# Sums of squares over 512 rows by split fp32r products instead of fp32 column products, in six norms of a two-block transformer kernel

## The reference

```
def rmsnorm(x, g):                      # EPS = 1e-6; the second block has EPS_2 = 1e-5
    x32 = x.astype(jnp.float32)
    y = x32 * lax.rsqrt(jnp.mean(x32 * x32, axis=-1, keepdims=True) + EPS)
    return (y * g.astype(jnp.float32)).astype(x.dtype)
...
x = x + jnp.concatenate([mix_out, mem_out], axis=-1) @ w_out
x = x + conv_ffn(rmsnorm(x, norm_ffn_g[l]), ffn_w_up[l], ffn_conv_w[l], ffn_conv_b[l], ffn_w_down[l])
...
def conv_ffn(h, w_up, conv_w, conv_b, w_down):
    u, g = jnp.split(h @ w_up, 2, axis=-1)
    g = causal_dwconv(g, conv_w, conv_b)
    return (jax.nn.silu(g) * u) @ w_down
```

## Time and profile before

| | us |
|---|---|
| runs | 1776.76, 1777.09, 1777.13; median 1777.09 |
| span of the profiled execution | 1775.3 |
| median less that span | 1.8 |
| TensorE (PE) busy | 1765.4 (99%) |
| VectorE (DVE) busy | 1273.6 (72%) |
| ScalarE (ACT) busy | 949.8 (53%) |
| GpSimd (POOL) busy | 204.9 (12%) |

### The profile page before, as it was taken

One profiled execution on the slowest core, in us unless ns is written; L12 is line 12 of the kernel. 1 busy time (PEld: TensorE's weight loads), 2 busy tenths in 40 slices (PEclk: granted clock), 3 DMA queues, 4 the chain that ended last, 5 costly groups with the idle time before them and its releaser, 6 DMA issues.

```text
span 1775.3 us, 26378 instructions
## 1 busy us (share of the span) xinstructions
PE 1765.4 (99%) x10758; PEld 1534.0 (86%) x10758; DVE 1273.6 (72%) x1773; ACT 949.8 (53%) x1440; POOL 204.9 (12%) x225
## 2 busy tenths in 40 slices
PE   9999999999999999999999999999999999999998
PEld 7877788999999887777899999978777889999997
DVE  6878567788786655656888787687767487766765
ACT  6645444655555544755555555552567455454454
POOL 0001220110111200002011110103001101111110
PEclk9999999999999999999999999999999999999999
DMA  6221223554545333212364554433221235555442
GB/s 249 72 92 64 71 95 107 152 138 139 143 123 139 103 132 110 96 48 85 107 173 114 154 129 141 109 119 106 73 96 48 97 106 145 141 140 145 107 140 74
DMA packets 61623, 205.19 MB, mean 116 GB/s; under 512 B 7344, under 2 KB 9520, under 8 KB 53184
## 3 DMA queue, kind: packets, MB, share of 16 engines
q1 hardware_dynamic: 38832, 162.55, 26.5%
q0 software_dynamic: 17280, 31.46, 10.0%
q10 hardware_dynamic: 5392, 9.51, 1.7%
HBM read 169.38 MB, written 2.13 MB: 97 GB/s over the span
## 4 chain that ended last, share of the span: by engine, by line
PE 96%; DVE 2%; ACT 1%; DMA 0%; SPq 0%; issue 0%; DVEq 0%; ACTq 0%
PE ps L1784 31%; PE ps L1451 21%; PE ps L1810 16%; PE ps L1373 7%; PE ps L1470 4%; PE ps L1833 2%; PE ps L1490 2%; PE ps L1597 2%; PE ps L1642 2%; PE ps L1622 2%; PE ps L1681 1%; PE ps L1662 1%; PE ps L1851 1%; PE ps L1414 1%; PE ps L1353 0%; DVE WL L2449 0%
## 5 line engine op out<-in xcount | busy, mean ns | idle before, releaser
L1784 PE MATMUL ps<-hH,WL 128*128 128x256 f32 x896 | 253.6, 283 | 0.0
L1784 PE MATMUL ps<-hL,WH 128*128 128x256 f32 x896 | 253.6, 283 | 0.0
L1784 PE MATMUL ps<-hH,WH 128*128 128x256 f32 x896 | 253.4, 283 | 0.0
L2471 DVE TENSOR_TENSOR WL<-raw,WH 128x1024 fp32r<-128x1024 f32 x138 | 168.3, 1221 | 116.6 <-ACT WH L1935 116.6
L2449 DVE TENSOR_TENSOR WL<-raw,WH 128x1024 fp32r<-128x1024 f32 (+1 forms) x138 | 167.6, 1253 | 91.8 <-ACT WH L1924 91.7
L1451 PE MATMUL ps<-hH,WH 128*128 128x512 f32 x544 | 215.3, 396 | 0.0
L1451 PE MATMUL ps<-hH,WL 128*128 128x512 f32 x544 | 212.0, 390 | 0.0
L1451 PE MATMUL ps<-hL,WH 128*128 128x512 f32 x544 | 211.9, 390 | 0.0
L3197 POOL DMA_DIRECT2D X<-sq x120 | 104.9, 967 | 862.0 <-ACT sq L1990 860.1
L1784 PE MATMUL ps<-TH,WL 128*128 128x256 f32 x672 | 190.2, 283 | 0.0
L1784 PE MATMUL ps<-TL,WH 128*128 128x256 f32 x672 | 190.2, 283 | 0.0
(11 more groups left out here) (418 smaller groups left out, 3869.0 us busy)
## 6 DMA issues: line engine op xcount, KB each, us to landing
raw<-in_wall SPq DMA_DIRECT2D x166, 512.0 KB, 4.2
raw<-in_wall SPq DMA_DIRECT2D x65, 1024.0 KB, 4.7
X<-sq POOLq DMA_DIRECT2D x120, 256.0 KB, 4.0
bias<-in_bias ACTq DMA_DIRECT2D x12, 256.0 KB, 2.9
raw<-in_wall SPq DMA_DIRECT2D x8, 256.0 KB, 6.1
X<-in_xt SPq DMA_DIRECT2D x8, 256.0 KB, 6.7
CB<-rows ACTq DMA_DIRECT2D x8, 256.0 KB, 3.4
out_y<-X SPq DMA_DIRECT2D x8, 256.0 KB, 2.2
```

Source lines behind the costliest of these rows:

```text
L1784: mm = e.matmul(ps[b][:, 256 * u:256 * u + 256], ww[:, p, 128 * u:128 * u + 128], x, start=(opens and p == 0 and u == 0 and n == 0), stop= ...
L2471: e.tensor_tensor(L, chunk_src(c), H.bitcast(F32), ALU.subtract).then_inc(*mark("wl", "c", c))
```

## The change

Six norms lose their column products. `acc` is split into a high and a low fp32r part (`row_split`: ScalarE copies `accH`, VectorE subtracts for `accL`), and TensorE multiplies a 128x128 tile of ones, `ones_r`, with both, summed in one bank of 128x512 (`row_sums`). ScalarE takes the root over 128x512 straight into Rsb, and VectorE the reciprocal of Rsb in place (`row_inverse`). Where columns are needed (mix0, kv, n1), VectorE makes them from Rsb: four products with the identity, each with a sum along the free axis (`row_columns`). The spreads and the copy of Rsb are gone. The accH and accL tiles lie where sq0 and sq1 do.

The order changes too. In the feed-forward parts the split takes the place of the old sums, and the new sums come after g1; the reciprocal follows at once (WHOLE 2) or after the next conversions (WHOLE 1). For kv the three steps fall on three tiles one after another, without the pause ahead of them. In mix0 the split lies between the halves of the conversion of unit 3. At the join both splits come before the first tile of dq, the sums after dq1 with one root and reciprocal, the second reciprocal and the columns after the second piece of dv.

```diff
     def rstd(i, eps):
-        norms.extend([None, ("rstd_rows", i, eps), None] if i in ("ffn0", "ffn1", "n2") else
-                     [None, ("rstd_first", i, eps), ("rstd_second", i)])
+        norms.extend([("row_split", i), ("row_sums", i, eps), ("row_inverse", i)])
...
         whole("g", 0, n)
-        put("rstd_first", st, 61 if i == 2 else 60)
+        put("row_split", st)
         put("wtS", i, 1)
         put("wtL", i, 1)
         put("wtB", i, 2)
         put("wtS", i, 2)
         whole("g", 1, n)
         done.add(n)
-        put("rstd_second", st)
+        put("row_sums", st, 61 if i == 2 else 60)
+        if WHOLE[i] == 2:
+            put("row_inverse", st)
...
         conv_ahead(len(UNITS))
+        if WHOLE[i] == 1:
+            put("row_inverse", st)
...
+    put("conv", 3, 0)
+    put("row_split", "mix0")
+    put("conv", 3, 1)
+    now["conv"] = 4
     tm(1, "memA", "mvA", "mvcp", ntt=2)
     put("gate_products", "A")
-    put("rstd_first", "mix0", 60)
-    norms.append(("rstd_second", "mix0"))
+    put("row_sums", "mix0", 60)
+    put("row_inverse", "mix0")
...
-    norms.extend([None, ("join_first",), ("join_second",)])
+    norms.extend([None, ("join_sums",), ("join_second",)])
     put("fence", "C")
     put("rope_load")
     put("chunk_bias")
+    put("join_split")
...
+            def row_sums(b, parts, key):
+                for n, x in enumerate(parts):
+                    mm = e.matmul(ps[b][:, :], ones_r[:, :], x[:, :], start=(n == 0), stop=(n == 1))
                 mm.then_inc(*mark(*key))
...
+                elif what == "row_split":
+                    w.wait_ge(*at("acc" + SQ_LAST[a[0]], a[0], 7))
+                    e.activation(accH[:, :], acc[:, :], ACT.Copy).then_inc(*mark("rowH", a[0]))
...
                     e.activation(Rsb[:, :], ps[BANK[("rs", a[0])]][:, :], ACT.Sqrt, bias=small[:, eps:eps + 1],
                                  scale=1.0 / 1024).then_inc(*mark("rsq", a[0]))
...
+            def row_low(low, whole, high, name):
+                w.wait_ge(*at("rowH", name))
+                e.tensor_tensor(low[:, :], whole[:, :], high[:, :].bitcast(F32), ALU.subtract).then_inc(
+                    *mark("rowL", name))
+            def row_columns(name):
...
+                for i in range(4):
+                    c = slice(128 * i, 128 * i + 128)
+                    e.tensor_tensor_reduce(diag[:, c], Rsb[:, c], ident, 1.0, 0.0, ALU.mult, ALU.add,
+                                           small[:, 4 + i:5 + i]).then_inc(*mark("rcol", name, i))
...
+                elif what == "row_inverse":
                     w.wait_ge(*at("rsq", a[0]))
+                    e.reciprocal(Rsb[:, :], Rsb[:, :]).then_inc(*mark("Rsb", a[0]))
+                    if a[0] in ("mix0", "kv"):
+                        row_columns(a[0])
...
+                elif what == "join_split":
+                    row_low(accL, acc, accH, "n1")
+                    row_low(acc2L, acc2, acc2H, "join")
+                elif what == "join_sums":
+                    w.wait_ge(*at("sums", "n1"))
+                    w.wait_ge(*at("sums", "join"))
+                    e.tensor_scalar(Rsb[:, :], ps[BANK[("rs", "n1")]][:, :], 1e-5, None, ALU.mult).then_inc(
+                        *mark("jsq1"))
+                    w.wait_ge(*at("jsq1"))
+                    e.tensor_tensor(Rsb[:, :], Rsb[:, :], ps[BANK[("rs", "join")]][:, :], ALU.add).then_inc(
+                        *mark("jsq"))
                     w.wait_ge(*at("rsq", "n1"))
+                    e.reciprocal(Rsb[:, :], Rsb[:, :]).then_inc(*mark("Rsb", "n1"))
+                elif what == "join_second":
                     w.wait_ge(*at("rsq", "join"))
+                    e.reciprocal(acc2[:, :], acc2[:, :]).then_inc(*mark("Rsb", "join"))
+                    row_columns("n1")
```

More of the change, by code:

```diff
@@ L1024, in program @@
         K = place("K", [128, 5, 128])
+        ones_r = place("ones_r", [128, 128], F32R)
         KB = place("KB", [128, 3, 128], BF16)
@@ L1028, in program @@
         diag = place("diag", [128, 512])
+        accH, accL = (place(f"acc{x}", [128, 512], F32R, offset=top[0] - 2048 * n) for x, n in (("H", 3), ("L", 2)))
         held_w = place("held3", [128, 2, 256], offset=top[0] - 2048)
@@ L1138, in program @@
         Tf = place("Tf", [128, 4, 256], offset=wino + 49152)
+        acc2H, acc2L = (place(f"acc2{x}", [128, 512], F32R, offset=wino + 81920 + 2048 * n)
+                        for n, x in enumerate("HL"))
         gw = place("gw", [128, 8, 32], offset=227840)
@@ L1526, in tensor @@
                         w.wait_ge(*at(*before))
-                    w.wait_ge(*at("acc" + SQ_LAST[a[0]], a[0], 7))
-                    sums(b, acc, 0, ("sums", a[0]))
-                elif what == "rstd_rows":
-                    b, before = bank(("rs", a[0]), ("rsq", a[0]))
-                    if before:
-                        w.wait_ge(*at(*before))
[L1535 to L1557, removed]
+                    w.wait_ge(*at("rowH", "ones"))
+                    w.wait_ge(*at("rowH", a[0]))
+                    w.wait_ge(*at("rowL", a[0]))
+                    row_sums(b, (accH, accL), ("sums", a[0]))
+                elif what == "join_sums":
+                    for name, parts, drain in (("n1", (accH, accL), ("rsq", "join")),
+                                               ("join", (acc2H, acc2L), ("jsq",))):
+                        b, before = bank(("rs", name), drain)
+                        if before:
+                            w.wait_ge(*at(*before))
+                        w.wait_ge(*at("rowH", name))
+                        w.wait_ge(*at("rowL", name))
+                        row_sums(b, parts, ("sums", name))
                 elif what == "gates_later":
@@ L2067, in scalar @@
                         e.activation(sq[k % 2][:, :], X[:, k, :], ACT.Square).then_inc(*mark("sqA", "mix0", k))
-                elif what == "rstd_first":
+                elif what == "row_split":
+                    w.wait_ge(*at("acc" + SQ_LAST[a[0]], a[0], 7))
+                    e.activation(accH[:, :], acc[:, :], ACT.Copy).then_inc(*mark("rowH", a[0]))
+                    if a[0] == "mix0":
+                        w.wait_ge(s_K if ev.sems else None, 16)
+                        e.activation(ones_r[:, :], ones, ACT.Copy).then_inc(*mark("rowH", "ones"))
+                elif what == "row_sums":
+                    eps = a[1]
                     w.wait_ge(*at("sums", a[0]))
                     w.wait_ge(*at("eps", 1))
[L2072 to L2078, removed]
                     for x in R_USED[a[0]]:
@@ L3290, in program @@
                   "last": [("fg", "g2", 21), ("fy", 2, 21)]}
-        RCOL_USED = {"mix0": [], "ffn0": [("vev", "vA", 2, 2), ("spread", "mix0")], "kv": [("spread", "ffn0")],
-                     "ffn1": [("vev", "vB", 2, 2), ("spread", "kv")], "n1": [("spread", "ffn1")],
-                     "n2": [("vev", "fv", 2, 1), ("spread", "n1")], "last": [("spread", "n2")]}
+        RCOL_USED = {"mix0": [], "kv": [("vev", "vA", 2, 2)], "n1": [("vev", "vB", 2, 2)],
+                     "last": [("vev", "fv", 2, 1)]}
         SQ_USED = {("ffn0", 1): [("cvD", "k", 5, 3)], ("ffn0", 2): [("cvD", "k", 4, 3)],
@@ L3310, in program @@
                 ROPE_AT.setdefault(n + 1 + NRAW, []).append((a[0], a[1]))
-        OD_BEFORE = {0: [("accD", "n1", 6), ("acc2", 6)], 1: [("accD", "n1", 7), ("acc2", 7)], 2: [("sums", "n1")],
-                     3: [("spread", "join")]}
+        OD_BEFORE = {0: [("sums", "n1")], 1: [("sums", "n1")], 2: [("sums", "n1")],
+                     3: [("rcol", "n1", 3)]}
         def norm_at(stage, u, x):
```

80 lines of the change are left out of this document (23 added, 57 removed).

## The result

The change makes the kernel slower: 1786.57 us (median of 4 runs, 1786.37 to 1787.06) against 1776.92 for the kernel before (4 runs beside it, 1776.66 to 1777.13), a ratio of 1.0054, 95% interval 1.0042 to 1.0067. The forecast was 1776.1, in a range of 1770.5 to 1780.5, so the measured time lies 6.1 us above the range.

What follows compares the result with a forecast made beforehand. TensorE's instruction stream was taken as the path. Net terms of -4.2 (mix0, ffn0, kv), +1.1 (ffn1), +0.7 (join) and +1.4 (n2) gave -1.0 us, so 1776.1 us against 1777.1, with a range of 1770.5 to 1780.5.

Steps and rivals of the forecast that it cites:

- The gross gain: TensorE's saving from cheaper norm products: 1.40 us in each of five norms, 2.7 at the join, 9.7 in all.
- no such row exists: Claim that the profile had no 128x512 reciprocal; 3.3 us was taken from the nearest row, 64x512 at 3.35.
- the bounds of 0.7 and 6.7: Limits in us for the 128x512 reciprocal: an ordinary VectorE pass, or a cost that counts partitions.
- the split and the root: Over 128x512: the split some 0.5 us on ScalarE and 0.6 on VectorE, the root another 0.58.
- The table load: Load of the root's table, paid behind the second TH copy in three feed-forward norms: 1.30 us, against 2.66 with the skill's drain.
- The first two waits of ffn1: TensorE waits 1.4 us for the weights' low part, then 1.0 us at the next stage's second product.
- mix0 ... at nothing: In mix0, ffn0 and kv the longer helper work costs TensorE no wait, leaving their gain at -4.2 us.
- so the rest dies out: After ffn1's two waits VectorE's 7.0 us of idle time absorbs its lag; loss 2.45, net +1.1 us.
- the second rival: VectorE's backlog does not die out, with added waits at 916.10 and its like in ffn0: +4.5, 1781.6 us; 12%.
- TensorE's next work after the dv products is the fp32 product that reads Gf: At the join TensorE reaches this product at 1203.1 and waits 3.5 us for Gf; net +0.7 us.
- ScalarE's chain behind it: In n2, conversion, Silu's table, two Silus, T7 and conversion make the fifth product 0.5 us late.
- The clock falls in a pause: Rival: during the wait for Gf the clock falls to 1.2 GHz, adding 2.9 us, to 1779.0; 8%.

Runs made afterwards that it cites:

- mix0_ln: Changed kernel with mix0's root and reciprocal made on ScalarE as exp(-0.5 ln(x)), so no long VectorE reciprocal there; 1785.96 us, ratio 1.0051.
- ffn1_late: Changed kernel with ffn1's reciprocal behind T's low part and the next unit's conversion instead of ahead of them; 1788.63 us, ratio 1.0066.
- join_late: Changed kernel with the join's second reciprocal and the columns behind the evictions U and Gf instead of ahead; 1780.96 us, ratio 1.0023.
- held_first: Changed kernel with ScalarE's copy of n2's first small product moved ahead of two weights' high parts and two Silus; 1783.74 us, ratio 1.0039.
- filled_two: Changed kernel with useless products added in TensorE's waits, 20 before dv's fourth piece and 17 before n2's third small product; 1782.32 us, ratio 1.0031.
- lnexp: Changed kernel with all six norms' root and reciprocal made on ScalarE as exp(-0.5 ln(x)), no reciprocal on VectorE; 1777.45 us, ratio 0.9999.
- after: The kernel with the whole change, against the kernel before; 1786.57 us, ratio 1.0054.
- n2_old: Changed kernel with the last feed-forward norm, n2, put back in its old form at its old places; 1781.80 us, ratio 1.0026.
- filled: Changed kernel with 20 useless products added in TensorE's join wait, ahead of dv's fourth piece; 1784.28 us, ratio 1.0041.

## Why the prediction was wrong

Net effect of each part on TensorE's shift, forecast and measured:

| part | forecast us | measured us |
|---|---|---|
| start | 0 | +0.1 |
| mix0, ffn0, kv | -4.2 | -0.1, -0.9, -1.4 |
| ffn1 | +1.1 | +2.2 |
| join | +0.7 | +4.4 |
| n2 | +1.4 | +5.8 |
| sum | -1.0 | +10.0 |

Of the 11.0 us between the sums, 4.6 are the clock, which the sum had at nothing, and 3.1 are waits that were longer than forecast (5.0 for 3.5 at the join; one of 4.4 for 2.8 in three pieces in n2). Nearly all of the rest is mix0 and ffn1.

**What held.** The gross gain (9.7; measured 9.5 by the shifts). The reciprocal's 3.35 us, though "no such row exists" was wrong: L3068 above is one, and with it the bounds of 0.7 and 6.7 were not needed. Also the split and the root within 0.15. The table load: it starts at 844.94 and the root at 846.24, again 1.30, so the drain that the Trainium skill ("ScalarE: Activation LUTs", "What ACT_TABLE_LOAD costs") adds is not to be seen. kv was without a wait, ffn0 had one of 0.24 and lost 0.5 of its gain. The first two waits of ffn1: 1.35 for 1.4 and 0.75 for 1.0.

**"mix0 ... at nothing".** The step followed the norm to the next weights and stopped there. VectorE and ScalarE stay behind for 55 us, up to a copy that TensorE wants in the memory attention with under 0.5 us to spare. mix0_ln shows it. The wait was 1.2 us.

**"so the rest dies out", ffn1.** There was a third wait, 0.77, for a held copy, earlier than the place at 916.10 that the second rival named, where TensorE did not wait. And the two that I had were no two independent places: ffn1_late moved the reciprocal, and the sum of 2.9 us stayed. The part came out 1.1 us dearer.

**"TensorE's next work after the dv products is the fp32 product that reads Gf", the join.** This step failed. The dv pieces need banks, and the fourth bank hangs on U, which I had in the list of late evictions and whose start I had within 0.6 us. I asked who reads the result of the late instruction and not who needs the bank that it empties. The wait was to begin at 1203.1 and end at 1206.6. It began at 1200.4 and ended at 1205.4: 5.0 instead of 3.5 us. join_late shows it, since with U ahead of the second reciprocal 0.7 are left.

**n2.** The fourth failed step: for the third product I looked at the weights (1.2 us) and costed "ScalarE's chain behind it" only for the fifth. The third product waits for a copy in that chain: 4.4 us. held_first shows it.

**"The clock falls in a pause" (8%).** This is the largest single miss: the sum had the clock at nothing. The rival's price, 2.9, was of the right size for one fall; it happened twice, 2.0 and 2.6 us by the shifts, 4.3 to 4.8 together by filled_two. I wrote that no row shows it in the middle of the kernel. But the rival hung on a wait that was in my own sum, and later runs had the clock fall around waits of 2.5 and 3.0: with one of 3.5 forecast, one in twelve was too low. The Trainium skill ("TensorE: Matmul & The Clock Gate", Part 1) has the clock halve after idle time, and the traces now agree: 0.50 around the waits of 5.0 and 4.4.

With the join and n2 at their measured 10.2 us instead of 2.1, the forecast would have been 1784.2.

## What to carry over

When an instruction gets longer on an engine off the critical path, follow everything behind it in that engine's queue by three questions: who reads it, who needs the PSUM bank or buffer that it empties, and what on another engine is queued behind something that waits for it; and follow it over as many stages as it takes until its results are back at their old times. Waits that have one backlog as their cause can be one sum, as in ffn1: moving a step within the queue joined them and took nothing off. A long wait costs more than its length, because the clock falls. Put the long instruction behind the evictions that free banks, and where there is no room on either helping engine, as in ffn1 and n2, keep the form that costs TensorE 1.4 us.

## What the runs showed of the hardware

In the profiled executions the granted clock stayed at 1.00 behind waits of TensorE of up to 1.7 us (held_first) and fell around waits of 2.5 (lnexp: 0.78 in the mean of 7 us), 3.0 (ffn1_late: 0.75 over 6.3 us), 4.4 and 5.0 (after: 0.50 over 6.6 and 6.8 us). Where the low stretch begins within the wait, part of it costs nothing: after, at the join, it is there from 1202.6 while the product comes at 1205.4, and that wait paid 2.0 us for it, the one of 4.4 us in n2 paid 2.6.

The same wait does not always cost the same. The join's was 4.8 to 5.0 us in after, held_first, ffn1_late, n2_old and mix0_ln; less the 2.5 that its part costs in filled, where the clock does not fall, the price of the fall by the shifts was 1.9, 2.6, 2.3, 1.6 and 1.4 us.

One VectorE sum over 128x128 with its product costs 0.21 us from start to start in a row of four, 0.8 to 0.9 for the four with the last one's end, where 1.1 was forecast.
